# Two of six adaLN vectors in the opening, the other four on VectorE during the even projections; values in two parts in the neighbourhood attention; first heads loaded a stage ahead

## The reference, cut to what matters

```python
mod_l = (jax.nn.silu(c) @ ada_w[layer] + ada_b[layer])[:, None, :]
mod_c = (jax.nn.silu(c_ctx) @ ada_w[layer] + ada_b[layer])[None, None, :]
sh1, sc1, g1, sh2, sc2, g2 = jnp.split(mod_l, 6, axis=-1)
...
h_l = modulate(x, norm1_g[layer], sh1, sc1)
...
x = x + g1 * (o_l @ w_out[layer])
x = x + g2 * sq_relu_mlp(modulate(x, norm2_g[layer], sh2, sc2), mlp_w1[layer], mlp_w2[layer])
```

## Time and profile before

| | us |
|---|---|
| median of 3 runs (3911.56 to 3914.55) | 3914.34 |
| the profiled execution's own time | 3916.25 |
| its span, first to last instruction | 3914.5 |
| PE busy | 3586.2 (92%) |
| DVE busy | 2002.1 (51%) |
| ACT busy | 1284.4 (33%) |
| POOL busy | 174.4 (4%) |
| granted TensorE clock, mean over the span | 0.951 |

### The profile page before, as it was taken

One profiled execution on the slowest core, in us unless ns is written; L12 is line 12 of the kernel. 1 busy time (PEld: TensorE's weight loads), 2 busy tenths in 40 slices (PEclk: granted clock), 3 DMA queues, 4 the chain that ended last, 5 costly groups with the idle time before them and its releaser, 6 DMA issues. The chain is left out here.

```text
span 3914.5 us, 47315 instructions
## 1 busy us (share of the span) xinstructions
PE 3586.2 (92%) x17690; PEld 2863.7 (73%) x17690; DVE 2002.1 (51%) x2873; ACT 1284.4 (33%) x2279; POOL 174.4 (4%) x178
## 2 busy tenths in 40 slices
PE   8798798797899999999988979799799889999999
PEld 2586565786788888888877768577577668888887
DVE  2456564786663444443445455588544363333333
ACT  2453243564431111111125445466433341111111
POOL 0210010000120000000001000000000020000000
PEclk9899799898999999999999979799899899999999
DMA  8335564422321222221214344333344311111112
GB/s 313 132 129 188 143 136 89 113 76 87 88 83 57 69 62 70 60 60 55 66 51 155 140 142 143 97 73 73 81 101 92 108 54 46 46 48 48 54 54 65
DMA packets 431360, 366.47 MB, mean 94 GB/s; under 512 B 103381, under 2 KB 374117, under 8 KB 426085
## 3 DMA queue, kind: packets, MB, share of 16 engines
q1 hardware_dynamic: 431205, 364.42, 32.6%
HBM read 276.67 MB, written 87.69 MB: 93 GB/s over the span
## 5 line engine op out<-in xcount | busy, mean ns | idle before, releaser
L2033 DVE SCALAR_TENSOR_TENSOR xT<-ps,mods,xT 128x1024 f32<-128x1024 f32 x192 | 189.4, 1014 | 426.0 <-PE ps L2247 426.0
L2247 PE MATMUL ps<-e_gh,e_w2h 128*128 128x512 f32 x1280 | 356.7, 376 | 5.9 <-DVE e_w2l L2492 3.6
L2247 PE MATMUL ps<-e_gl,e_w2h 128*128 128x512 f32 x1280 | 352.8, 373 | 0.0
L2247 PE MATMUL ps<-e_gh,e_w2l 128*128 128x512 f32 x1280 | 352.2, 373 | 0.0
L2542 DVE TENSOR_TENSOR e_plain<-e_plain 128x1280 f32<-128x1280 f32 (+1 forms) x64 | 86.9, 1358 | 482.1 <-ACT e_plain L2407 482.1
L2247 PE MATMUL ps<-e_hl,e_w1h 128*128 128x512 f32 (+1 forms) x1200 | 327.2, 370 | 0.0
L2247 PE MATMUL ps<-e_hh,e_w1l 128*128 128x512 f32 (+1 forms) x1200 | 327.2, 370 | 0.0
L2247 PE MATMUL ps<-e_hh,e_w1h 128*128 128x512 f32 (+1 forms) x1200 | 327.1, 370 | 0.0
L2407 ACT ACTIVATE e_plain<-ps 128x1280 f32<-128x1280 f32 (+1 forms) x64 | 72.7, 1135 | 761.5 <-PE ps L2247 757.4
L2247 PEld LDWEIGHTS ps<-e_gh,e_w2h 128*128 128x128 f32 x1280 | 224.9, 190 | 55.5 <-DVE e_gl L2546 8.0
L2247 PEld LDWEIGHTS ps<-e_gh,e_w2l 128*128 128x128 f32 x1280 | 226.1, 190 | 43.6
(11 more groups left out here) (349 smaller groups left out, 7445.0 us busy)
## 6 DMA issues: line engine op xcount, KB each, us to landing
e_raw<-in_mlp_w SPq DMA_DIRECT2D x64, 512.0 KB, 4.1
e_raw<-in_mlp_w SPq DMA_DIRECT2D x128, 256.0 KB, 2.9
aw<-in_ada_w SPq DMA_DIRECT2D x12, 2048.0 KB, 9.0
rstd<-in_ada_w SPq DMA_DIRECT2D x64, 384.0 KB, 3.4
e_raw<-in_w_out SPq DMA_DIRECT2D x40, 512.0 KB, 3.9
qkC<-pc_stage SPq DMA_DIRECT2D x72, 192.0 KB, 2.7
hT<-pb_hb SPq DMA_DIRECT2D x10, 1024.0 KB, 5.4
pa_hb<-hT SPq DMA_DIRECT2D x10, 1024.0 KB, 5.0
```

Source lines behind the costliest of these rows:

```text
L2033: ins = k.nc.vector.scalar_tensor_tensor(out=x, in0=ps, scalar=k.mods[:, layer, gate, bass.ds(n, 1), w], in1=x, op0=ALU.mult, op1=ALU.add)
L2247: mm = pe.matmul(k.ps[:, SB * (e % 2) + b, 0:n], w[:, e % 2, f], m[:, f, c0:c0 + n], start=(f == 0 and x == 0), stop=(f == nf - 1 and x == 2))
```

## The change

- The opening makes the first two vectors (four halves). The token tiles follow one another behind the first half. The squares are taken for a chunk of 512 tokens at a time and two feature tiles at once, and the sum over partitions is two products in place of one.
- `project` has a new argument `vectors`: pb makes the vectors 2 and 3 of layer 0, pa 4 and 5. Each vector comes in two groups of 512 columns, each group in eight slices of 128x512 through the ring `raw`. Per slice DVE adds the slice times a scalar to two accumulators (`vector_part`, two operations); behind a group's last slice PE sums over partitions with eight small float32 products (`vector_sums`) and DVE adds the bias (`vector_sum`). `slices_at` spreads the slices: two per job, in pb in four jobs out of six, in pa in all of sixteen jobs. In pa the score banks MB go from 4 to 3.
- `attend` takes `split` apart from `parts`: ad now has it too, with LAG 3 in place of 2.
- `Ahead` tiles at the end of SBUF hold the first head of ab, aa and ad. They are loaded by `load` in the stage before: ab's in pa at job 10, aa's in ab behind the loads of its first pair, ad's in ac. v of ab and ad, and k of aa's second map, are still loaded in the stage itself.

```diff
-        N_HALVES = 6 * D_MODEL // HALF
+        N_HALVES = OPENING_VECTORS * D_MODEL // HALF
...
-        steps = [("x", t) for t in range(XB)]
-        for n in range(N_HALVES):
-            steps += [("ada", n)] + [("x", t) for t in (XB + 2 * n, XB + 2 * n + 1) if t < NT]
-
-        X_DONE, SUM_AT = 3, 8
+        steps = [("x", t) for t in range(XB)] + [("ada", 0)] + [("x", t) for t in range(XB, NT)] + [("ada", n) for n in range(1, N_HALVES)]
+        PAIRS = KT // 2
+        squared_at, summed_at = {0: (0,), 1: (1, 2)}, {1: (0,), 2: (1, 2)}
...
-    RAW, LAG, MB, TB = 6, 2, 4, 4
+    RAW, LAG, TB, GC = 6, 2, 4, 512
+    MB, AB, ACCS = (3, 3, 2) if vectors and not keeps_h else (4, 7, 1)
+    NW, NG = len(slices), len(vectors) * D_MODEL // GC
+    PERIOD, FIRST = (N - U - 2) // NG if NG else 0, U
...
+    def slices_at(n):
+
+        g, y = (n - FIRST) // PERIOD, (n - FIRST) % PERIOD
+        if n < FIRST or g >= NG:
+            return range(0)
+        busy = PERIOD - 2 * (2 - ACCS)
+        return range(g * KT + min(KT, y * KT // busy), g * KT + min(KT, (y + 1) * KT // busy))
...
+                def fetch_vectors(a):
+                    x = NW + a
+                    if a < RAW:
+                        sp.wait_ge(s.wlo, x - RAW + 1)
+                    else:
+                        sp.wait_ge(s.aacc, 2 * (a - RAW + 1))
+                    sp.dma_start(raw[:, x % RAW], a_dram[a_group[a // KT], a % KT]).then_inc(wr[x % RAW], 16)
...
+                    if ahead_of is not None and n == N // 2:
+                        ahead_of.load(sp)
...
+                def vector_sums(g):
+                    pe.wait_ge(s.aacc, 2 * (g + 1) * KT)
+                    if g:
+                        pe.wait_ge(s.modd, g)
+                    for c in range(GC // P):
+                        for w in range(2):
+                            mm = pe.matmul(k.ps[:, AB, 2 * c + w:2 * c + w + 1], a_acc[g % ACCS][:, w, c * P:(c + 1) * P], k.ones[:, 0:1],
+                                           start=True, stop=True)
...
+                def vector_part(a):
+                    x, g, f = NW + a, a // KT, a % KT
+                    dve.wait_ge(wr[x % RAW], 16 * (x // RAW + 1))
+                    if f:
+                        dve.wait_ge(s.aacc, 2 * a)
...
+                            part = nc.vector.scalar_tensor_tensor(out=here, in0=raw[:, x % RAW], scalar=k.sil2[:, f, w:w + 1],
+                                                                  in1=here, op0=ALU.mult, op1=ALU.add)
...
+                    for a in slices_at(n) if NG else ():
+                        vector_part(a)
+                    for g in group_after(n, 2) if NG else ():
+                        vector_sum(g)
...
-    split = parts == "three"
+    three = parts == "three"
     PT, LAG = 4, 3 if split else 2
...
+    def load(self, sp):
+        if self.sink is not None:
+            sp.dma_start(self.sinks[:], self.sink.unsqueeze(0).broadcast_to([P, NA_HEADS])).then_inc(self.tab, 16)
...
+        self.loader(sp, 0, 0, (self.q[:], self.k_[:], None, self.q_ext[0:HD], self.k_ext[0:HD]), self.near, self.far)
+        if self.bias_loader is not None:
+            self.bias_loader(sp, 0, 0, self.raw[:], self.rawT[:], self.bias)
```

More of the change, by code:

```diff
@@ L41 @@
 NEXT_BANK = 5
+SBUF_END = 229344
+VECTORS, OPENING_VECTORS = 6, 2
 SLICE = 4
@@ new lines, with __init__, load @@
+class DiffAhead(Ahead):
+    def __init__(self, k, st, name, end):
+        super().__init__(k, st, name, end)
+        self.q = [self.tile(f"q{m}", [P, TOK], F32R) for m in range(2)]
+        self.k0, self.v = self.tile("k0", [P, 2, TOK], F32R), self.tile("v", [P, NT, 2 * HD])
+    def load(self, sp):
+        k = self.k
+        sp.dma_start(f32(self.q[0][:]), k.qkA[0]).then_inc(self.near, 16)
+        for part in range(2):
+            for half in range(2):
+                sp.dma_start(f32(self.k0[half * HD:(half + 1) * HD, part]), k.qkA[8, part * HD:(part + 1) * HD]).then_inc(self.near, 16)
+        sp.dma_start(f32(self.q[1][:]), k.qkA[1]).then_inc(self.far, 16)
+        sp.dma_start(self.v[:], k.vA.rearrange("(t p) d -> p t d", p=P)[:, :, 0:2 * HD]).then_inc(self.far, 16)
@@ L266, in turn_rows, with sums @@
                     mm.then_inc(s.colT, 1)
[L268 to L271, removed]
+                def sums(c):
+                    if c == 0:
+                        pe.wait_ge(s.xcpA, NT)
+                        pe.wait_ge(s.xcpD, NT)
+                    pe.wait_ge(s.acc, (c + 1) * (PAIRS - 1))
+                    for a in range(2):
+                        mm = pe.matmul(k.ps[:, TB + c, 0:chunks[c][1]], k.ones[:], both(c)[:, a], start=(a == 0), stop=(a == 1))
                     mm.then_inc(s.sum, 1)
@@ L280, in _ @@
                             turn_rows(n - 1)
-                        if n == SUM_AT:
-                            sums()
+                        for c in summed_at.get(n, ()):
+                            sums(c)
                 turn_rows(N_HALVES - 1)
@@ L1279, in steps_of_head, with attend @@
     return out, blocks
-def attend(k, name, pieces, heads, load_head, parts, v_width, mix, mix_col, sink=None, bias=None, beside=None):
+def attend(k, name, pieces, heads, load_head, parts, split, v_width, mix, mix_col, sink=None, bias=None, beside=None, ahead=None, ahead_of=None):
     nc = k.nc
@@ L1453, in pair @@
                             beside.loads(s, sp)
+                        if ahead_of is not None:
+                            ahead_of.load(sp)
                     for p in range(2):
@@ L1816, in attend_diff @@
         TB, OB = 6, 7
+        assert nc.sbuf_base <= ahead.end
         def scores(b):
```

324 lines of the change are left out of this document (223 added, 101 removed).

## The result

| | before | changed |
|---|---|---|
| median of 7 runs each, us | 3914.34 (3908.39 to 3918.85) | 3930.6 (3927.94 to 3938.45) |
| profiled execution, its span | 3916.25, 3914.5 | 3932.05, 3928.9 |
| PE, DVE, ACT busy | 3586, 2002, 1284 | 3566, 2154, 1337 |
| granted TensorE clock | 0.951 | 0.942 |

What follows compares the result with a forecast made beforehand. PE was busy 92%, but its wait chain reached only the last stage, so stages were priced separately: -47 + 12 + 14 - 11.5 - 11.5 - 8 - 11 = -63, from 3916.25 to 3853, median 3851; range 3836 to 3876.

Steps and rivals of the forecast that it cites:

- The opening, -47: Opening: eight of twelve adaLN halves go from PE, less reload and sum costs; 47 us less, bounds -50 and -43.
- called itself wrong from 40: Failure sign: pb and pa together growing by under 15 or over 40 us.
- pb, +12: pb: PE's sums add 7.2 us and DVE's uneven slices 5; 12 us more, bounds +7 and +25.
- the average just fits: pb, per two token tiles: DVE's 31.3 us with slices against PE's 31.7.
- +7.2 on an engine that is the limit: pb: four times eight small float32 products for the sums add 7.2 us to PE.
- The bound of +25: pb's upper bound: the full 3.5 us of each six-slice tile, five times.
- pa, +14: pa: two slices a job make DVE the limit, 7.2 us a job against PE's 6.37; bounds +8 and +20.
- disappear in PE's new idle time: pa: PE's sums over partitions cost nothing, as DVE sets the pace.
- First heads: Starts of ab, aa and ad: heads loaded ahead save 11.5, 11.5 and 8 us.
- ad's steps, -11: ad: three fp32r value products replace one float32 product; 11 us less, bounds -16 and +5.
- The rule on this operation: pb and pa: half throughput would add about 20 and 26 us, total near 3898; the forecast instead followed the trace.
- the slower one: Rival, pb and pa slices: both projections VectorE-bound at 2.9 us a slice, total 3939; chance 0.04.

Runs made afterwards that it cites:

- Experiments 1: Changed kernel with PE's sums over partitions and DVE's bias addition one job later in pb and pa: 3892.7 us, ratio 0.9942 to the kernel before.
- 2: Changed kernel with pb's slices moved to the jobs without heads, four in each of eight: 3873.8 us, ratio 0.9898 to the kernel before.
- 8: Changed kernel with later sums, pb's slices in jobs without heads, next first heads loaded at the last pair, q and k before v: 3828.4 us, ratio 0.9786.

## Why the prediction was wrong, step by step

**The opening, -47**: right, -45.0. The sum gave an end at 67; it ends at 68.9. PE's rows there: the second half begins at 40.21 behind 6.69 us of waiting for its load, where 37.5 was said.

```profile
16.74 9.85 PE L319 MATMUL ps<-aw,sil 128*2 128x512 f32 x16 [3.49 <-DMA aw<-in_ada_w]
...
40.21 8.36 PE L319 MATMUL ps<-aw,sil 128*2 128x512 f32 x16 [6.69 <-DMA aw<-in_ada_w]
...
68.52 0.41 PE L328 MATMUL ps<-ident_sb,mrow 2*128 2x2 f32 x4 [0.33 <-ACT mrow L378]
```

Pb and pa together grew by 103 us, where the prediction called itself wrong from 40.

**pb, +12**: this step failed, by 61 us. Its two prices were right: a multiply and add of 512 columns takes 0.75 us, the sums 1.8 us at full clock. What failed is the sentence that "the average just fits", and then the sums' cost as "+7.2 on an engine that is the limit", PE's own time only. The sum put the work of a period side by side, 31.3 for DVE and 31.7 for PE. That holds only if PE may run ahead. The prediction saw that slices "lie in four jobs of six" and that POOL's scaling holds DVE, and put 5 us on both, but it never asked what the *wait* of the sums stands behind. What the runs showed in its place, in the period of 48.9 us read above: 10.6 us of PE waiting for DVE, at the sums and at a turn, and 6.6 us of a lower clock on products and sums behind it. An order of instructions with the waits beside it shows this without a trace: sums for the slices of job n - 1, right behind the products of n. The bound of +25 was made from DVE's overload too, so it could not hold the case. Experiments 1, 2 and 8 show the size of each part: with both placed well, pb is 7.5 us above before, at the lower bound of +7 that was "PE's share alone".

**pa, +14**: the mechanism was right (7.07 us a job against 7.2 said), the four waits at the sums were missing: +30.1, and +13.3 without them. The claim that the sums "disappear in PE's new idle time" is the failed line: PE stands up to 4.8 us ahead of them, its next products come late, and DVE then waits 4.9 us for its reduce.

**First heads**: ab's and ad's starts came as said, 11.5 and 8.1 us earlier; aa's `lam4` 14.1 us earlier against 11.5, within the bounds. The failed line is the last of that part: the loads "now run in pa, ab and ac beside PE-bound work". In ab they met the scatter of the bias table on full DMA engines, and one wait of 9.3 us took most of the gain back. Pricing a moved load needs the DMA share of the stretch into which it is moved; in the kernel before it is 0.61 from 500 to 560 us in ab as a mean, and 1.15 in the profile's count from 512 to 518.

**ad's steps, -11**: -5.5 measured, within the bounds. The size was low (17.6 is there to be had), and the waits for k took 8.7. That the change also turned the order of v and k was in its diff, and was not priced.

**The rule on this operation**: the Trainium skill, Vector Engine (DVE) Microarchitecture Reference, "Points that are easy to get wrong", says that this form runs at half throughput with two non-bf16 sources in SBUF. With that page's slope this is an estimated 1.14 us for 512 columns. The trace disagrees: in pa all 56 operations with two float32 operands in SBUF take 743 to 754 ns. With that rule the total would have been put near 3898, nearer to the result and for a reason that is not there.

**The rivals**: the slower one named the right place, both projections, and a total of 3939 near the measured one. But its mechanism, a slice of 2.9 us, was not there. The same number from another cause is no confirmation; "VectorE is overloaded" would have led to taking slices away, and the cure was to put them elsewhere. The rival that fitted, a wait behind which PE's run-ahead is lost, was not among them. The chance of 0.94 for faster had no room for it.

## What to carry to other kernels

When work is moved onto an engine with room, the average load decides little. Write down, for each new wait, what its engine has queued behind it, and how far the producer is behind at that very place. Here a sum that closes a group belonged one job later than the first place where it was allowed (38 us), and filler work where its engine would wait, not ahead of what another one waits for (57 us). Loads fetched ahead need a stretch in which the DMA engines are not full; here the last pair of the stage before was one.

## What the runs showed of the hardware

A pause of PE can cost more than its length. In pb's period of 48.9 us, 10.6 us of idle time came with a granted clock of 0.83, and the lower level cost 4.9 us on products and turns and 1.7 on the sums, over 0.6 of the pauses' length once more. Not every pause does: after one of 2.72 us, ending at 228.52, the clock stayed at 1.00. The same 16 rows of the sums take 3.57 us in that period and 1.84 where PE never stops.

DVE's slice operations take up to 2.1 us longer beside POOL's scaling: a row of four takes 5.01 us at 195.24, 2.93 otherwise. The first of a group, a multiplication only, has a median of 1.55 us in pb and 0.48 in pa:

```profile
L828 DVE TENSOR_SCALAR pb_aacc<-pb_wraw,sil x8: 480/1550/2623, 125.7 to 270.2; 128x512 f32<-128x512 f32 x8
L828 DVE TENSOR_SCALAR pa_aacc<-pa_wraw,sil x4: 479/480/482, 367.5 to 428.7; 128x512 f32<-128x512 f32 x4
```

(min, median, max in ns, then first and last start.)

POOL's row beside the first case (`pb_hfull`, start and length first) ends at 198.18, where DVE's second operation would have begun at about 195.98; the 2.2 us between are the excess of 2.08.

```profile
195.40 2.78 POOL L891 TENSOR_TENSOR pb_hfull<-xT,rstd 128x1024 f32<-128x1024 f32 x1 [18.47 <-DVE pb_hb L766]
```

The Trainium skill, SBUF — State Buffer, "Who interferes with whom", says that the two engines share a port pair under an exclusive lock, that a DVE instruction with two inputs in SBUF contends with a GpSimd instruction that reads SBUF, and that the order of issue decides which one blocks. By that rule DVE's second operation stood until POOL's ended, and the trace agrees.
